# Two seven-product sets a pair, with side products a pair ahead, in the gate/up stage of a hybrid decoder layer

## The reference, cut to what matters

```python
h = rms_norm(x, ffn_norm_w[layer], NORM_EPS)
a = jax.nn.silu(jnp.einsum('bsd,df->bsf', h, w_ffn_gate[layer])) * jnp.einsum('bsd,df->bsf', h, w_ffn_up[layer])
x = x + jnp.einsum('bsf,fd->bsd', a, w_ffn_down[layer]).astype(x.dtype)
```

## Time and profile before

| what | us |
|---|---|
| median of three runs | 2068.26 (2067.58 to 2069.1) |
| span of the profiled execution | 2065.0 |
| PE busy in it | 2058.4 |
| DVE busy in it | 1531.8 |
| ACT busy in it | 1126.8 |

### The profile page before, as it was taken

One profiled execution on the slowest core, in us unless ns is written; L12 is line 12 of the kernel. 1 busy time (PEld: TensorE's weight loads), 2 busy tenths in 40 slices (PEclk: granted clock), 3 DMA queues, 4 the chain that ended last, 5 costly groups with the idle time before them and its releaser, 6 DMA issues.

```text
span 2065.0 us, 28156 instructions
## 1 busy us (share of the span) xinstructions
PE 2058.4 (100%) x9584; PEld 1698.2 (82%) x9584; DVE 1531.8 (74%) x1859; ACT 1126.8 (55%) x1441; POOL 158.5 (8%) x195
## 2 busy tenths in 40 slices
PE   9999999999999999999999999999999999999999
PEld 8888877778888888888888888888888888888887
DVE  6777866665757777777667887897777777787866
ACT  5444555555556666666655454555555555555553
POOL 1121000000012222222000000000000000000000
PEclk9999999999999999999999999999999999999999
DMA  7656675564565655656565647666766767656574
GB/s 247 199 179 204 194 214 169 167 174 142 184 204 185 183 183 183 183 183 183 172 192 185 211 162 239 192 205 205 213 193 198 219 205 215 196 184 219 181 241 156
DMA packets 209802, 399.77 MB, mean 194 GB/s; under 512 B 15873, under 2 KB 21426, under 8 KB 209730
## 3 DMA queue, kind: packets, MB, share of 16 engines
q1 hardware_dynamic: 205346, 384.79, 59.6%
q0 software_dynamic: 3776, 13.70, 2.6%
q10 hardware_dynamic: 608, 0.34, 0.1%
HBM read 387.18 MB, written 2.16 MB: 189 GB/s over the span
## 4 chain that ended last, share of the span: by engine, by line
PE 96%; DMA 2%; DVE 2%; ACT 0%; issue 0%; SPq 0%; DVEq 0%; POOL 0%; ACTq 0%; POOLq 0%
PE acc L2041 79%; PE side L2128 6%; PE acc L2128 4%; PE side L2057 3%; PE side L2341 1%; DMA w_raw<-in_w_ffn_down 1%; DVE w_lo L1833 1%; PE side L2196 1%; DVE w_raw L1754 0%; DMA x_row<-in_x 0%; PE side L2347 0%; PE acc L2057 0%; PE side L2270 0%; DMA w_raw<-in_w_ffn_up 0%; ACT w_hi L1034 0%
## 5 line engine op out<-in xcount | busy, mean ns | idle before, releaser
L1075 DVE TENSOR_TENSOR w_lo<-w_raw,w_hi 128x1024 fp32r<-128x1024 f32 x332 | 416.1, 1268 | 251.7 <-ACT w_hi L576 250.4
L576 ACT ACTIVATE w_hi<-w_raw 128x1024 fp32r<-128x1024 f32 x332 | 347.9, 1057 | 372.5 <-PE acc L2041 319.4
L2041 PE MATMUL acc<-w_hi,h_hi 128*128 128x512 f32 x1248 | 498.5, 399 | 0.2
L2041 PE MATMUL acc<-w_hi,h_lo 128*128 128x512 f32 x1248 | 487.2, 390 | 0.0
L2041 PE MATMUL acc<-w_lo,h_hi 128*128 128x512 f32 x1248 | 486.0, 389 | 0.0
L984 ACT ACTIVATE w_hi<-w_raw 128x1024 fp32r<-128x1024 f32 x209 | 220.4, 1060 | 215.5 <-PE acc L2041 132.7
L1749 DVE TENSOR_TENSOR w_lo<-w_raw,w_hi 128x1024 fp32r<-128x1024 f32 x209 | 252.8, 1223 | 93.9 <-ACT w_hi L984 87.7
L2041 PEld LDWEIGHTS acc<-w_hi,h_hi 128*128 128x128 f32 x1248 | 234.5, 188 | 51.0 <-issue 5.6
L2041 PEld LDWEIGHTS acc<-w_hi,h_lo 128*128 128x128 f32 x1248 | 234.2, 188 | 50.2
L2041 PEld LDWEIGHTS acc<-w_lo,h_hi 128*128 128x128 f32 x1248 | 234.7, 188 | 48.1 <-issue 1.9
L2041 PE MATMUL acc<-w_hi,x2T_hi 128*128 128x512 f32 x528 | 207.3, 393 | 0.1
(11 more groups left out here) (435 smaller groups left out, 3099.4 us busy)
## 6 DMA issues: line engine op xcount, KB each, us to landing
w_raw<-in_w_in SPq DMA_DIRECT2D x320, 512.0 KB, 4.3
w_raw<-in_w_ffn_gate SPq DMA_DIRECT2D x88, 512.0 KB, 4.3
w_raw<-in_w_ffn_up SPq DMA_DIRECT2D x88, 512.0 KB, 4.6
w_raw<-in_w_ffn_down SPq DMA_DIRECT2D x88, 512.0 KB, 4.7
w_raw<-in_w_ssm_proj SPq DMA_DIRECT2D x64, 512.0 KB, 4.6
w_raw<-in_w_attn_proj SPq DMA_DIRECT2D x32, 512.0 KB, 3.7
w_raw<-in_w_out SPq DMA_DIRECT2D x32, 512.0 KB, 5.0
acs_b<-acs_scratch POOLq DMA_DIRECT2D x16, 512.0 KB, 6.9
```

The lines of the kernel that those rows point to most:

```text
L576: nc.scalar.activation(w_hi[:, r], w_raw[:, n % RING], ACT.Copy).then_inc(hi_ready, 1)
L1075: nc.vector.tensor_tensor(w_lo[:, r], w_raw[:, n % RING], w_hi[:, r].bitcast(F32), ALU.subtract).then_inc(lo_ready, 1)
L2041: done = nc.tensor.matmul(acc[p][:, t], a[:, k0 + kk, cut], w[:, r, kk], start=first and kk == n == 0, stop=last and kk == UK - 1 and n == 2)
```

## The change

Sets 0 and 1 both take seven products (called A and B), sets 2 and 3 stay plain (g0 to g3 gate, u0 to u3 up). P1, P5, P6 and P7, which go to side, are computed for the next pair, while P2, P3 and P4 belong to the current one. Both sets add up in the side banks before anything is combined. The weights of the side products are loaded into six buffers of their own (side_raw), up to two pairs ahead, and their sums are formed there; the third sum is a POOL DMA that reads the second up block from HBM and adds it to the first. So a set takes five loads and one such DMA. The combinations are written into the accumulators before the pair's own matmuls, which then all add to them: P1 into acc[0][:, 0] and the negated mids into acc[0][:, 1] by ScalarE, the sum of P5 and mids into both halves of acc[1] by VectorE. Silu and the multiply then read the accumulators directly. PE waits for these seeds (acc00_seeded, acc01_seeded, acc1_seeded) and, ahead of P1A, for product_lo of the same pair, since the transposes now use banks 2 and 3.

The head (FFN_HEAD) computes pair 0 with plain units throughout, beside the side products of pair 1. The last pair (FFN_TAIL) has no side products. Nine pairs (FFN_PAIR) lie between. x2 is stored to HBM in the head (two DMAs of 1 MB), since side_raw takes part of its place, and loaded again in four DMAs in the down stage. Both sets' stationary sums are made in the head. The diff, cut to its core:

```diff
+FFN_SEVENS = (0, 1)
+FFN_PLAIN = 2
+FFN_HEAD = ("G0", "G1", "U0", "U1", "G2", "G3", "U2", "U3",
+            "g0", "P1A", "g1", "P5A", "g2", "P6A", "g3", "P7A", "u0", "P1B", "u1", "P6B", "u2", "P7B", "u3", "P5B")
+FFN_PAIR = ("P2A", "P2B", "g0", "P4A", "g1", "P1A", "P4B", "g2", "P5A", "P6A", "g3", "P7A",
+            "P3A", "u0", "P1B", "u1", "P6B", "P3B", "u2", "P7B", "u3", "P5B")
+FFN_TAIL = tuple(name for name in FFN_PAIR if name[:2] not in ("P1", "P5", "P6", "P7"))
...
+def ring_loads(names):
+    return [name for name in names if name[0] != "P" or name[:2] in ("P2", "P3")]
...
+        side_raw = [[at(f"side_raw{s}{n}", kb, [P, UK, CW]) for n, kb in enumerate(places)]
+                    for s, places in enumerate(((123, 167, 127), (183, 187, 171)))]
...
+            def ffn_side(s, n, column):
+                first = 2 * UK * FFN_SEVENS[s]
+                source, row = ((w_ffn_gate, first), (w_ffn_up, first), (w_ffn_up, first + UK))[n]
+                src = source[0, row * P:(row + UK) * P, bass.ds(column, CW)]
+                sp.dma_start(side_raw[s][n][:], src.rearrange("(k p) n -> p k n", p=P)).then_inc(side_in[s][n], 16)
...
+            sp.wait_ge(x2_out, 16 * D // CW + 2 * 16)
+            sp.wait_ge(x2_T, 4)
+            sp.wait_ge(x2_ss, 2 * TT)
+            ffn_side(1, 0, CW)
+            ffn_side(1, 1, CW)
...
+                sp.wait_ge(t4_ready, sums.now(-1))
+                ffn_ring(names, "g2", column)
+                sp.wait_ge(t4_ready, sums.now())
+                ffn_ring(names, "g3", column)
+                if not last:
+                    remainder(names, "P4A")
+                    ffn_side(0, 2, column + CW)
...
+            def back(c):
+                part = slice(c * CW, (c + 1) * CW)
+                sp.dma_start(x2[:, :, part], x2_dram[:, part].rearrange("(t p) d -> p t d", p=P)).then_inc(x2_back, 16)
...
+                elif name[:2] == "P5":
+                    act.wait_ge(t1_ready, sums.now(1 + "AB".index(name[2])))
+                elif name[:2] == "P6":
+                    act.wait_ge(t2_ready, sums.now(1 + "AB".index(name[2])))
+                elif name[:2] == "P7":
+                    act.wait_ge(t3_in["AB".index(name[2])], pairs.now() * 16 + 16)
+                else:
+                    act.wait_ge(t4_ready, sums.now(2 * ahead - 1 + "AB".index(name[2])))
+                act.wait_ge(mm_done, unit.now(1 - RING))
...
+                        for t in range(TT):
+                            last = nc.scalar.activation(gate_f[:, t], acc[0][:, t], ACT.Silu, scale=x2_scale[:, t:t + 1])
+                        last.then_inc(gate_f_ready, 1)
...
+                    if "P1B" in names and at == names.index("P1B"):
+                        act.wait_ge(mm_done, unit.now(-LEAD))
+                        if not head:
+                            act.wait_ge(acc1_seeded, pairs.now())
+                        nc.scalar.activation(mids[:, 0], side[:, 2], ACT.Copy).then_inc(p1_ready, 1)
+                        act.wait_ge(gate_f_ready, pairs.now(1))
+                        nc.scalar.activation(acc[0][:, 0], side[:, 2], ACT.Copy).then_inc(acc00_seeded, 1)
+                    if "P7B" in names and at == names.index("u3"):
+                        act.wait_ge(mids_ready, pairs.now(1))
+                        nc.scalar.activation(acc[0][:, 1], mids[:, 1], ACT.Copy, scale=-1.0).then_inc(acc01_seeded, 1)
...
+            def first_sum(s):
+                dve.wait_ge(side_in[s][1], pairs.now() * 16 + 32)
+                nc.vector.tensor_tensor(side_raw[s][0][:], side_raw[s][0][:], side_raw[s][1][:], ALU.add).then_inc(t1_ready, 1)
+            def second_sum(s):
+                dve.wait_ge(side_in[s][2], pairs.now() * 16 + 32)
+                dve.wait_ge(t1_ready, sums.now(s + 1))
+                nc.vector.tensor_tensor(side_raw[s][2][:], side_raw[s][2][:], side_raw[s][0][:], ALU.add).then_inc(t2_ready, 1)
+            def fourth_sum(s):
+                dve.wait_ge(t2_ready, sums.now(s + 1))
+                nc.vector.tensor_tensor(side_raw[s][2][:], side_raw[s][2][:], w_raw[:, s], ALU.add).then_inc(t4_ready, 1)
...
+                    if not head and at == 0:
+                        dve.wait_ge(mm_done, unit.now(-LEAD))
+                        dve.wait_ge(mids_ready, pairs.now())
+                        dve.wait_ge(a_ready, pairs.now())
+                        nc.vector.tensor_tensor(acc[1][:], side[:, 0].unsqueeze(1).broadcast_to([P, TT, CW]), mids[:],
+                                                ALU.add).then_inc(acc1_seeded, 1)
...
+                    if sides and at == names.index("P1A") - LEAD:
+                        first_sum(0)
+                    if sides and at == names.index("P6A") - LEAD - 2:
+                        second_sum(0)
+                    if sides and at == names.index("P1B") - LEAD:
+                        first_sum(1)
+                    if sides and at == names.index("P6B") - LEAD - 1:
+                        second_sum(1)
+                    if sides and at == names.index("P6B"):
 
                         dve.wait_ge(mm_done, unit.now(-LEAD))
-                        dve.wait_ge(p1_ready, i + 1)
+                        dve.wait_ge(p1_ready, pairs.now(1))
+                        link(nc.vector.tensor_tensor(mids[:, 0], side[:, 1], mids[:, 0], ALU.subtract))
+                    if sides and at == len(names) - LEAD:
+                        fourth_sum(0)
+                    if sides and at == names.index("P7B"):
+                        dve.wait_ge(mm_done, unit.now(-LEAD))
                         if not head:
-                            dve.wait_ge(a_T, i)
-                        link(nc.vector.tensor_tensor(up_f[:, 0], side[:, 1], gate_f[:, 0], ALU.subtract))
-                        link(nc.vector.tensor_tensor(up_f[:, 1], up_f[:, 0], side[:, 3], ALU.subtract))
-                    if at == AFTER7 - 1:
-                        nc.vector.tensor_tensor(up_f[:, 0], side[:, 0], up_f[:, 0], ALU.add)
-                        nc.vector.tensor_tensor(gate_f[:, 1], side[:, 0], up_f[:, 1], ALU.add).then_inc(mids_free, 1)
-                    if at == AFTER7:
-                        dve.wait_ge(mm_done, unit.now(1 - LEAD))
-                        nc.vector.tensor_tensor(gate_f[:, 0], acc[0][:, 0], gate_f[:, 0], ALU.add)
-                        nc.vector.tensor_tensor(up_f[:, 1], acc[0][:, 1], up_f[:, 1], ALU.subtract).then_inc(gates_summed, 1)
-                        dve.wait_ge(gates_summed, i + 1)
-                        nc.vector.sem_inc(acc_free[0], 1)
-                    if at == OPERANDS - 2:
-                        dve.wait_ge(mm_done, unit.now(1 - LEAD))
-                        dve.wait_ge(mids_free, i + 1)
-                        nc.vector.tensor_tensor(up_f[:, 0], acc[1][:, 0], up_f[:, 0], ALU.add)
-                        link(nc.vector.tensor_tensor(gate_f[:, 1], acc[1][:, 1], gate_f[:, 1], ALU.add))
-                        nc.vector.sem_inc(acc_free[1], 1)
-                if head:
-                    dve.wait_ge(x2_rstd, 1)
-                dve.wait_ge(gate_f_ready, i + 1)
-                nc.vector.scalar_tensor_tensor(out=up_f[:, 0], in0=up_f[:, 0], scalar=x2_scale[:, 0:1], in1=gate_f[:, 0],
-                                               op0=ALU.mult, op1=ALU.mult)
-                nc.vector.scalar_tensor_tensor(out=up_f[:, 1], in0=gate_f[:, 1], scalar=x2_scale[:, 1:2], in1=up_f[:, 1],
-                                               op0=ALU.mult, op1=ALU.mult).then_inc(a_ready, 1)
-                raw.step(RAWS)
-
-            raw = Tally()
+                            dve.wait_ge(acc01_seeded, pairs.now())
+                        nc.vector.tensor_tensor(mids[:, 1], mids[:, 0], side[:, 3], ALU.subtract).then_inc(mids_ready, 1)
+                    if sides and at == len(names) - LEAD + 1:
+                        fourth_sum(1)
+                    if at == names.index("u3"):
+                        dve.wait_ge(mm_done, unit.now(-LEAD))
+                        dve.wait_ge(gate_f_ready, pairs.now(1))
+                        for t in range(TT):
+                            last = nc.vector.scalar_tensor_tensor(out=gate_f[:, t], in0=acc[1][:, t], scalar=x2_scale[:, t:t + 1],
+                                                                  in1=gate_f[:, t], op0=ALU.mult, op1=ALU.mult)
+                        last.then_inc(a_ready, 1)
...
+                row = 2 * UK * FFN_SEVENS[s] + UK
+                src = w_ffn_up[0, row * P:(row + UK) * P, bass.ds(i * CW + CW, CW)]
+                pool.dma_start(side_raw[s][1][:], src.rearrange("(k p) n -> p k n", p=P), accum_op=ALU.add).then_inc(t3_in[s], 16)
...
+                    if name == "P2A":
+                        pe.wait_ge(acc00_seeded, pairs.now())
+                    if name == "g0" and not head:
+                        pe.wait_ge(acc01_seeded, pairs.now())
+                    if name == "P1A" and not head:
```

(55 more changed lines are left out.)

386 lines of the change are left out of this document (229 added, 157 removed).

## The result

The changed kernel takes 2082.1 us (median of 4 runs, 2080.89 to 2082.74) against 2067.92 for the kernel before (4 runs): ratio 1.007, 95% interval 1.0056 to 1.0084. It is slower by 0.7%. The forecast was 2067.9 with a range of 2059 to 2078, so both are missed. The profiled execution took 2080.89 us, its span is 2079.2, 14.2 more than before.

The account below looks back on a forecast made before the run. Gate/up was taken as bound by TensorE's number of matmuls. Head +12.7, nine pairs -1.8, last pair -12.3, down +1.0 gave -0.4: span 2064.6, with 3.3 to the median 2067.9 us, range 2059 to 2078.

Parts of the forecast that it names:

- The matmuls, -12.2: Gate/up stage: fewer matmuls on PE, 451.5 against 463.8 us, 12.2 us less, the whole of what can be won.
- VectorE's run and the wait ahead of P1A, 1.3 us: Middle pairs: a 14.4 us VectorE run before product_lo makes PE wait 1.3 us in each of nine pairs.
- Rival A: Middle pairs: the wait at P1A does not come, nine times 1.3 us come off, 2056 us; chance 0.12.
- The seed of acc[1], 1.135 against 1.32: VectorE's 1024-element write into PSUM: taken as 1.135 us, upper bound two passes of 0.66.
- both ends are hidden: Pairs: the accumulate from HBM lands in 4.5 to 6.9 us; P7A has 10 us, P7B 7.3, so no wait.
- rival B: ScalarE's rounding of P7B: side B's accumulate lands late; 8.0 us gives +8 over nine pairs, 2076; chance 0.18.
- The head, 57.0: First part of gate/up: 57.0 us against 44.3, +12.7, with 0.6 us waiting at g2; bounds 0 and 4.
- The last pair, 30.9: Tail of gate/up: 30.9 us against 43.2, -12.3, with no P1A and so no wait.
- Down, +1.0: Down projection: four x2 loads among the weight loads cost 1.0 us; bounds 0 and 6.7.
- The range: Whole kernel: 2059 to 2078 us, taking in most of rival B and cutting Rival A.
- rival C: Head and down: one-time costs near their upper ends, +3 to +8 us; chance 0.06.
- From span to median, +3.3: Whole kernel: the median of three runs, 2068.26, is 3.3 us above the profiled span, added to the forecast span.

Follow-up runs that it names:

- e3_plain: The changed kernel with POOL's third-sum DMA as a plain copy from HBM, without the addition: 2071.08 us.
- e5_p1b: The changed kernel with P1B directly behind P7A, so first sum B and its accumulate are issued earlier: 2072.91 us.
- e10_p7next: e6_two plus e4_back, with PE's wait for acc[1] moved to U0 and P7A placed behind P1B: 2054.47 us, ratio 0.9935.
- e4_back: The changed kernel with x2 loaded back half in the last pair, half at position 1 of the down stage: 2077.88 us.
- e2_order: The changed kernel with VectorE's product_lo one operand earlier and the seed of acc[1] moved behind later operands: 2079.86 us.
- e6_two: The changed kernel with the diffs of e5_p1b and e2_order together: 2070.61 us.

## Why the prediction was wrong, by its own steps

- **The matmuls, -12.2: right.** Without waits the stage is 12.1 us shorter.
- **VectorE's run and the wait ahead of P1A, 1.3 us: right.** The run is 14.40 us long against 14.4. The row says 1.35 of idle time, 1.5 by the starts of the matmuls, with the run late; with the accumulate out of the way it is 1.03, 1.2 by the starts, and the period is 43.0 against 43.05 (e3_plain, e5_p1b). Rival A, no wait there, is false.
- **The seed of acc[1], 1.135 against 1.32: right.** 1.14. The Trainium skill's fixed cost of 125 ns on PSUM against 60 on SBUF (Perfetto Trace Analysis, Optimizing Scalar/DVE Operations) does not show in the write either: the row for the seed has 1.23, its neighbours 1.22.
- **The accumulate, "both ends are hidden": this step failed.** I bounded its landing between 4.5 us, an accumulate whose source was SBUF, and 6.9, a plain load from DRAM, as if reading HBM and adding were alternatives. The form has both, and took 7.4 us in this kernel and 7.5 to 8.2 in the experiments. The slack of 7.3 was also counted from the end of first sum B, with 0.2 left for POOL at most (rival B decides from 7.1), and POOL's instruction starts 0.63 us after that end. 7.4 + 0.6 against 7.3 is the 0.7 us that each period is longer. This is rival B, at its place (ScalarE's rounding of P7B) and with its count of nine pairs; its price was given as 8 us from a landing of 8.0, and it cost 6.8 in the periods and 0.9 more at the first g0 of the pairs. Its chance, 0.18, was too low for a form that no row of the trace showed and a slack of 0.4 us over the upper bound.
- **The head, 57.0: this step failed.** Its work and VectorE's order were right (56.78 in e10_p7next), but I took the head to begin where the out projection ends. The wait for acc[0] and acc[1] ahead of its first unit stood in the code that I read; acc[1] is still being read out there. It costs 4.5 us by the starts of the matmuls (4.4 of idle time) and, through the clock, 1.6 more; the 0.6 us that I had at g2 did not come. The upper bound of 4 for the head was meant for a late store of x2, which did not happen.
- **The last pair, 30.9: right** (31.21, and 30.78 without waits).
- **Down, +1.0: too small,** +2.4, inside its bounds of 0 and 6.7. Where the loads find no slack they are felt: 2.1 us of waits that are gone with e4_back. The kernel before itself had 0.7 us of such waits, among them. One execution does not fix the term further, since the stage differs by up to 3.2 us between kernels with the same loads.
- **The range.** Rival B and costs of the head and the down stage (rival C) came together, +7.6, +5.65 and +1.4. I had treated them as cases that exclude each other; each alone is within 2078, the sum is not.
- **From span to median, +3.3: partly luck.** Each execution on record is some 1.6 us above its own span (2080.89 and 2079.2 for the changed kernel). The rest came from a profiled execution of the kernel before that was faster than its median; the profiled one of the changed kernel happened to be so too, and the miss is 14.6 us by the spans and 14.2 by the medians.

## What to carry to other kernels

Where a stage is bound by one engine and all else is hidden, the order is the design: the same work took a span of 2079 or 2052 us by the places of two products, two VectorE operations and the x2 loads, and by one semaphore wait, and each wait that went made room for the next. Give an operation whose form is not in any trace the sum of the costs of its parts as an upper bound, and a place in the order that can bear it. At the seam to the stage before, read what each wait is for: a wait for two buffers where the first use needs one can idle the bound engine, and the profile may call it nothing but "issue"; look then for what another engine finished just before.

## What the runs showed of the hardware

- A 512 KB DMA from POOL's queue that reads HBM and adds to SBUF landed in 7.4 to 8.2 us (median of a stretch); the same without the addition in 4.4; the one with an SBUF source, in the kernel before, in 4.5. By the queue's rows an accumulate from HBM is 272 packets (5168 for 19) and 2.9 us of all 16 engines (13.3% of 415 us); the plain copy is 144 packets and 1.9 us (row below, of e3_plain); the accumulate from SBUF is 144 packets (1440 for 10) and 2.8 us. So the slow form differs from the other accumulate in its packets, and not in the engines' time. Whether the number of packets makes the 3 us, and what moves the landing between 7.4 and 8.2, was not tried.

```profile
q0 software_dynamic: 2736, 9.96, 8.5%
```

- POOL's own instruction takes 1.20 us for the accumulate from HBM (in every kernel that has it), 0.88 for the one from SBUF (before) and 0.72 for the plain copy (e3_plain).
- An idle time of 4.4 us on TensorE was followed by eight matmuls at the lower clock, 1.6 us, and idle times of 4.9 to 5.5 us at the same place by 8 to 13 of them (e2_order to e6_two). Ten idle times of 1.05 to 1.35 us in 395 us left the granted clock at 1.00.
